# Hybrid streaming encoder on one core: where a norm's last step and statistics run, and the order of the router's products

## The chip, the cores and the metric

One core of a Trainium2 chip runs the whole program in one launch. The metric is the device time of an execution in microseconds (us). The kernel before took 1324.36 us, the median of three runs (1321.24 to 1324.84). Engines are called TensorE (PE), VectorE (DVE), ScalarE (ACT), GpSimd (POOL) and SyncE (SP), as in the profile's rows.

## The reference

One layer on 256 prompt rows and 64 sample rows of 1024 channels, all in f32. A mixing sublayer (attention and a convolution branch side by side) is followed by a layer norm, a router that chooses 4 of 32 experts for each row, the experts, and a second layer norm:

```python
x = layer_norm(DN_ALPHA * x + mix @ w_out + b_out, ln1_g, ln1_b)
logits = (x @ w_router + b_router)
top_val, top_idx = lax.top_k(logits, TOP_K)
gate = jax.nn.softmax(top_val, axis=-1)
# for each expert e and the rows xe that chose it:
gt = jnp.minimum(xe @ w_gate[e] + b_gate[e], SWIGLU_LIMIT)
up = jnp.clip(xe @ w_up[e] + b_up[e], -SWIGLU_LIMIT, SWIGLU_LIMIT)
h = gt * jax.nn.sigmoid(SWIGLU_ALPHA * gt) * (up + 1.0)
yb = h @ w_down[e] + b_down[e]
# ff: each row's four yb, weighted by gate, summed
y = layer_norm(DN_ALPHA * x + ff, ln2_g, ln2_b)

def layer_norm(x, g, b):
    mu = x.mean(-1, keepdims=True)
    var = jnp.square(x - mu).mean(-1, keepdims=True)
    return ((x - mu) * lax.rsqrt(var + LN_EPS)) * g + b
```

The weights of the 32 experts are 12.6 MB each and are read once.

## The kernel before

The rows are held in three tiles: tile 0 (prompt rows 0 to 127), tile 1 (128 to 255) and tile 2 (the 64 sample rows, laid out as two halves of 512 channels on 128 partitions). Each engine runs an instruction list of its own; named semaphores connect them, and an engine goes through its list strictly in order.

**Router.** VectorE ends the first norm of the tiles in the order 2, 0, 1 (`x1_ready`). TensorE turns each tile with transposes (`turn_x1`, L1313), ScalarE copies the turned tile (`x1T_a`), and TensorE multiplies it by the router's weights (`logits`, L1324) in the order 0, 2, 1. `keep_clock` (L1331) issues products whose result nobody reads, each with two instructions of 256 columns. VectorE's `picked` (L901 to L910) takes the four best of each row, for the tiles 0, 2, 1. Then TensorE counts the rows of each expert (L1356, L1363), VectorE makes the ranks and `at_visit` (L948), and TensorE makes three rows of the order of visits out of it (L1415 to L1419, `order_mm`). VectorE turns these into tables: `rounds_ready` (L958) is what the head of TensorE's loop reads, `tables_done` (L972) what SP, GpSimd, ScalarE and VectorE read. Between these steps TensorE gathers the rows of the first block (`gather(sel0, ...)`, L1378; tiles 0, 1 and 2 are summed in one bank), and turns the gates (L1424).

**Experts.** A visit takes one expert's weights, in 6 buffers of 4 MB (two each for gate, up and down). For each block of 32 rows TensorE runs the gate products (L1388), the up products (L1388), the gather of the next block, the down products (L1464) and the `combine` of the block before (L1405, L1407), whose result VectorE adds to `yacc` (L994, `yadd`). SP waits for `tables_done` and loads the experts half by half (`load_half`, L250) in the order of the table; a half is issued when TensorE has done with what stood in it (`gate_half`, `gate_done` and so on). Visit 0 and visit 1 are loaded before the router is done.

**Tail.** After the last block, `combine(total, tt)` for the three tiles, VectorE's sums, and the second norm. For tile 0 and tile 1 VectorE makes the statistics (`var2`, L1043 and L1045), ScalarE the root (`std2`, L689), VectorE the reciprocal (`rstd2`, L1054) and (x - mean) * g (`scaled2`, L1049). Tile 0's last step is split: ScalarE multiplies by rstd (L693, `unit2`) and GpSimd adds b (L546, `y0_ready`). Tile 1's and tile 2's last steps are VectorE's (L1074, L1080). The tile 1 sum is L1060, `yadd` count total * 3 + 5. ln2's g and b come by DMA into rows 0, 1, 5 and 6 of the weight buffer `WG[0]` (`ln2_in`). SP issues the outputs in one list:

```python
for tt in range(2):
    sp.wait_ge(sem(f"y{tt}_ready"), 1)
    sp.dma_start(y_prompt[0, P * tt:P * tt + P, :], WG[0][:, 2 + tt, :])   # L410
sp.wait_ge(sem("y2_ready"), 1)
for half in range(2):
    sp.dma_start(split(y_sample[0])[:, :, half, :], ...)                   # L413
```

Of the kernel before, what the change touches and what calls it, by code (L numbers as in the profile page):

```python
# [5 lines left out]
ALU = mybir.AluOpType  # L6
ACT = mybir.ActivationFunctionType
# [7 lines left out]
P = 128  # L15
D = 1024
# [18 lines left out]
Q = P // SLOTS  # L35
# [19 lines left out]
def encoder_step(nc, x_prompt, x_sample, cache_k, cache_v, state_conv, w_in, b_in, rel_bias, w_att_o,  # L55
# [22 lines left out]
    with ctx:  # L78
# [5 lines left out]
        PS = ctx.enter_context(nc.psum_tensor("PS", [P, 8, 512], F32))  # L84

        def view(off, *dims, rows=P):
            n = 1
            for d in dims:
                n *= d
            ap = SB[0:rows, off:off + n]  # L90
            if len(dims) == 2:
                ap = ap.rearrange("p (a b) -> p a b", a=dims[0])
            if len(dims) == 3:
                ap = ap.rearrange("p (a b c) -> p a b c", a=dims[0], b=dims[1])
            return ap
# [69 lines left out]
        M0 = S0 + 5120  # L165
        tin = view(M0, 256)
        xg = view(M0 + 256, KC, SLOTS)
        hT = view(M0 + 512, KC, SLOTS)
# [70 lines left out]
        def sem(name):  # L239
            if name not in sems:  # L240
                sems[name] = ctx.enter_context(nc.semaphore(name))
            return sems[name]
# [37 lines left out]
        def _(sp):  # L280
# [127 lines left out]
            for tt in range(2):  # L408
                sp.wait_ge(sem(f"y{tt}_ready"), 1)
                sp.dma_start(y_prompt[0, P * tt:P * tt + P, :], WG[0][:, 2 + tt, :]).then_inc(sem("y_out"), 16)  # L410
# [10 lines left out]
        def _(pool):  # L421
# [122 lines left out]
            pool.wait_ge(sem("ln2_in"), 96)  # L544
            pool.wait_ge(sem("unit2"), 1)
            pool.tensor_tensor(WG[0][:, 2, :], WG[0][:, 2, :], WG[0][:, 1, :], ALU.add).then_inc(sem("y0_ready"), 1)  # L546

        @block.scalar
        def _(act):  # L550
# [135 lines left out]

            for tt in range(3):
                act.wait_ge(sem("var2"), tt + 1)
                act.activation(rstd[:, tt:tt + 1], mv[:, tt, 1:2], ACT.Sqrt, bias=eps_c).then_inc(sem("std2"), 1)  # L689
                if tt == 0:  # L690
                    act.wait_ge(sem("scaled2"), 1)
                    act.wait_ge(sem("rstd2"), 1)
                    act.activation(WG[0][:, 2, :], WG[0][:, 2, :], ACT.Copy, scale=rstd[:, 0:1]).then_inc(sem("unit2"), 1)  # L693

        @block.vector
        def _(dve):
            n = [0]

            def link(ins):  # L700

                n[0] += 1
                ins.then_inc(sem("dve_chain"), 1)
                dve.wait_ge(sem("dve_chain"), n[0])
# [333 lines left out]

            def var2(tt):

                dve.wait_ge(sem("yadd"), total * 3 + (4 + tt))
                for s in range(2):
                    ins = dve.bn_stats(stats[:, tt, 6 * s:6 * s + 6], yacc[:, D * tt + 512 * s:D * tt + 512 * s + 512])  # L1043
                link(ins)
                dve.bn_aggr(mv[:, tt, :], stats[:, tt, :]).then_inc(sem("var2"), 1)  # L1045
                dve.wait_ge(sem("var2"), tt + 1)

            def scaled2(tt):
                dve.scalar_tensor_tensor(WG[0][:, 2 + tt, :], yacc[:, D * tt:D * tt + D], mv[:, tt, 0:1], WG[0][:, 0, :],  # L1049
                                         ALU.subtract, ALU.mult).then_inc(sem("scaled2"), 1)  # L1050

            def rstd2(tt):
                dve.wait_ge(sem("std2"), tt + 1)
                dve.reciprocal(rstd[:, tt:tt + 1], rstd[:, tt:tt + 1]).then_inc(sem("rstd2"), 1)  # L1054

            add_tile(total, 0)
            var2(0)
            dve.wait_ge(sem("comb_mm"), total * 3 + 2)
            y1 = yacc[:, D:2 * D].rearrange("p (q n) -> p q n", q=Q)
            dve.scalar_tensor_tensor(y1, PS[:, 0:4, 0:256], gcol[:, 1:2], y1, ALU.mult, ALU.add).then_inc(sem("yadd"), 1)  # L1060
            dve.wait_ge(sem("ln2_in"), 96)
            scaled2(0)
            rstd2(0)
            var2(1)
            add_tile(total, 2)
            y2 = yacc[:, 2 * D:2 * D + 512]
            dve.wait_ge(sem("yadd"), total * 3 + 6)
            link(dve.bn_stats(stats[:, 2, 0:6], y2))
            halves_aggregated("var2", 3)
            scaled2(1)  # L1070
            rstd2(1)
            dve.wait_ge(sem("scaled2"), 2)
            dve.wait_ge(sem("rstd2"), 2)
            dve.scalar_tensor_tensor(WG[0][:, 3, :], WG[0][:, 3, :], rstd[:, 1:2], WG[0][:, 1, :], ALU.mult, ALU.add).then_inc(sem("y1_ready"), 1)  # L1074

            v = WG[0][:, 4, 0:512]
            link(dve.scalar_tensor_tensor(v, y2, mv[:, 2, 0:1], WG[0][:, 5, 0:512], ALU.subtract, ALU.mult))
            rstd2(2)
# [5 lines left out]
        def _(pe):  # L1084
# [253 lines left out]
            logits(0).then_inc(sem("logit_mm"), 1)  # L1338
            keep_clock(2)
            pe.wait_ge(sem("x1T_a"), TURN_PLACE[2])  # L1340
# [71 lines left out]
            pe.wait_ge(sem("sel0_ready"), 1)  # L1412
            gather(sel0, range(2))
            pe.wait_ge(sem("at_visit_ready"), 1)
# [4 lines left out]
            pe.matmul(PS[0:1, 6, 128:128 + NV], ident[0:1, 0:1], later, start=False, stop=True).then_inc(sem("order_mm"), 1)  # L1419
            gather(sel0, range(2, 3)).then_inc(sem("gath_mm"), 1)  # L1420
            pe.wait_ge(sem("gates_ready"), 1)
# [58 lines left out]
            combine(total, 2)  # L1480

# [25 lines left out]
```

## Time and profile before

| | |
|---|---|
| median of 3 runs | 1324.36 us (1321.24 to 1324.84) |
| profiled execution, its own time | 1322.88 us |
| its span (first to last instruction) | 1321.2 us |
| TensorE busy, share of the span | 1250.5 us, 95% |
| VectorE busy | 617.6 us, 47% |
| ScalarE busy | 202.3 us, 15% |
| GpSimd busy | 140.6 us, 11% |
| read from HBM | 455.14 MB |
| granted TensorE clock, mean | 0.987 |

The spans and all times of rows are those of the profiled execution. A matmul of f32 stands as two instructions in the profile, and as many weight loads. The page cuts the span into 40 equal slices of 33 us; its lines of digits give the busy share in tenths, and one gives GB/s. "PEclk" is the granted clock of TensorE, 1.00 for 2.4 GHz and 0.50 for 1.2 GHz.

### The profile page before, as it was taken

How to read it: one execution, taken by the hardware profiler on the slowest of the kernel's cores; microseconds unless marked ns; L12 is line 12 of the kernel's file. 1: busy time of each engine (PE TensorE's matmuls, PEld its weight loads, DVE VectorE, ACT ScalarE, POOL GpSimd, SP SyncE). 2: the span in 40 equal slices, each digit the busy share in tenths (PEclk: the TensorE clock that was granted, in tenths of full speed). 3: DMA queues.
4: the chain of work that ended last, by engine and by line, in shares of the span. 5: the costliest groups of instructions: out<-in, count | busy, mean ns of one | idle time of the engine just before them, and what ended most of it. 6: DMA issues, size and time to landing. Idle time of an engine off the chain costs nothing.

```text
span 1321.2 us, 41429 instructions
## 1 busy us (share of the span) xinstructions
PE 1250.5 (95%) x16750; PEld 721.7 (55%) x16751; DVE 617.6 (47%) x1156; ACT 202.3 (15%) x380; POOL 140.6 (11%) x466
## 2 busy tenths in 40 slices
PE   8999999999999989799999999999999799999994
PEld 6777676476645545345555555555555345555552
DVE  0369995473236433344344334443444234434445
ACT  1111112343002101011111111111111111111111
POOL 1930000000001000011001100110001001100110
PEclk9999999999999999899999999999999999999997
DMA  9333334652898999999999999999999999999995
GB/s 312 105 111 123 127 127 149 164 173 83 324 416 355 428 428 428 428 428 429 429 429 429 429 429 428 429 429 429 429 429 429 429 429 429 429 429 428 429 428 209
DMA packets 69652, 459.72 MB, mean 348 GB/s; under 512 B 18284, under 2 KB 22108, under 8 KB 45017
## 3 DMA queue, kind: packets, MB, share of 16 engines
q1 hardware_dynamic: 69336, 459.03, 84.8%
q10 hardware_dynamic: 289, 0.33, 0.1%
q8 instruction: 16, 0.26, 0.1%
q14 instruction: 11, 0.09, 0.0%
HBM read 455.14 MB, written 4.73 MB: 348 GB/s over the span
## 4 chain that ended last, share of the span: by engine, by line
PE 87%; DMA 9%; DVE 2%; issue 1%; ACT 1%; POOL 0%; POOLq 0%; SPq 0%; ACTq 0%; DVEq 0%
PE PS L1388 28%; PE PS L1464 15%; PE PS L1105 13%; DMA SB<-in_w_down_dram 9%; PE PS L1378 6%; PE PS L1405 5%; PE PS L1280 3%; PE PS L1213 3%; PE PS L1168 2%; PE PS L1290 2%; PE PS L1407 2%; PE PS L1124 1%; PE PS L1134 1%; PE PS L1455 1%; PE PS L1395 1%
## 5 line engine op out<-in xcount | busy, mean ns | idle before, releaser
L1388 PE MATMUL PS<-SB 128*32 128x256 f32 x7424 | 429.1, 383 | 36.3 <-issue 15.5
L1388 PEld LDWEIGHTS PS<-SB 128*32 128x32 f32 x7424 | 236.1, 110 | 214.1 <-issue 52.6
L1464 PE MATMUL PS<-SB 128*32 128x256 f32 x3712 | 215.8, 384 | 7.4 <-DMA SB<-in_w_down_dram 7.2
L994 DVE SCALAR_TENSOR_TENSOR SB<-PS,SB 128x1024 f32<-128x1024 f32 x176 | 193.6, 1100 | 7.2 <-PE PS L1405 2.9
L1006 DVE TENSOR_SCALAR PS<-PS 128x256 f32<-128x256 f32 x58 | 25.1, 433 | 337.2 <-PE PS L1395 337.2
L1105 PE MATMUL PS<-SB 128*128 128x320 f32 x640 | 172.8, 433 | 1.3 <-ACT SB L586 1.3
L1464 PEld LDWEIGHTS PS<-SB 128*32 128x32 f32 x3712 | 115.4, 111 | 89.8 <-DVE SB L1021 10.2
L1105 PEld LDWEIGHTS PS<-SB 128*128 128x128 f32 x640 | 121.4, 190 | 51.9 <-issue 1.5
L745 DVE SCALAR_TENSOR_TENSOR SB<-SB 128x350 f32<-128x350 f32 x240 | 118.6, 573 | 0.0
L684 ACT COPY SB<-PS 128x256 f32<-128x256 f32 x58 | 21.6, 372 | 603.6 <-PE PS L1464 603.6
L1378 PE MATMUL PS<-SB 128*32 128x256 f32 (+1 forms) x1416 | 96.6, 386 | 0.0
L1405 PE MATMUL PS<-SB 32*128 32x256 f32 x944 | 84.0, 426 | 0.6 <-ACT SB L684 0.6
L1013 DVE TENSOR_SCALAR PS<-PS 128x256 f32<-128x256 f32 x58 | 25.1, 433 | 121.9 <-PE PS L1395 121.9
L535 POOL CAST SB<-SB 96x1 bf16 x58 | 10.7, 184 | 664.2 <-PE PS L1455 664.0
L682 ACT ACT_TABLE_LOAD x58 | 74.4, 1283 | 6.6 <-DVE SB L972 5.5
L1378 PEld LDWEIGHTS PS<-SB 128*32 128x32 f32 (+1 forms) x1416 | 33.7, 107 | 53.7 <-issue 43.1
L1405 PEld LDWEIGHTS PS<-SB 32*128 32x128 f32 x944 | 37.0, 183 | 38.0 <-issue 37.9
L682 ACT ACTIVATE SB<-PS 128x256 f32<-128x256 f32 x58 | 22.3, 385 | 165.9 <-DVE PS L1006 165.9
L568 ACT ACTIVATE SB<-PS,SB 128x320 f32 x40 | 21.1, 528 | 142.5 <-PE PS L1105 142.5
L1213 PE MATMUL PS<-SB 128*128 128x320 f32 x128 | 38.0, 442 | 0.0
L1034 DVE TENSOR_SCALAR SB<-PS,SB 128x320 f32<-128x320 f32 x58 | 32.0, 551 | 12.8 <-issue 12.8
L1008 DVE TENSOR_TENSOR SB<-SB,PS 128x256 f32<-128x256 f32 x58 | 24.4, 421 | 26.2 <-ACT SB L682 26.2
(245 smaller groups left out, 894.8 us busy)
## 6 DMA issues: line engine op xcount, KB each, us to landing
SB<-in_w_gate_dram SPq DMA_DIRECT2D x64, 2048.0 KB, 18.4
SB<-in_w_up_dram SPq DMA_DIRECT2D x64, 2048.0 KB, 24.0
SB<-in_w_down_dram SPq DMA_DIRECT2D x64, 2048.0 KB, 27.1
SB<-in_w_in_dram SPq DMA_DIRECT2D x13, 2048.0 KB, 7.9
SB<-in_w_pw_dram SPq DMA_DIRECT2D x2, 2048.0 KB, 8.6
SB<-in_w_att_o_dram SPq DMA_DIRECT2D x2, 2048.0 KB, 7.7
SB<-in_w_out_dram SPq DMA_DIRECT2D x2, 2048.0 KB, 9.9
SB<-in_w_in_dram SPq DMA_DIRECT2D x4, 512.0 KB, 7.6
```

Of the source, the lines that this page charges most:

```text
L682: act.activation(tin, PS[:, 0, 0:256], ACT.Sigmoid, scale=SW_ALPHA).then_inc(sem("sig"), 1)
L745: dve.scalar_tensor_tensor(yc[:, c, :], uext[:, c, bass.ds(k, CONVN)], dwT[:, c, bass.ds(k, 1)], yc[:, c, :], ALU.mult, ALU.add).then_inc( ...
L994: dve.scalar_tensor_tensor(y, ps, gcol[:, tt:tt + 1], y, ALU.mult, ALU.add).then_inc(sem("yadd"), 1)
L1034: dve.tensor_scalar(scat, PS[:, 0, 0:T], slotcol[:, bass.ds(done + b, 1)], None, ALU.is_equal).then_inc(sem("scat_ready"), 1)
L1105: ins = pe.matmul(PS[:, t, 0:T], ring[s][:, c, P * t:P * t + P], xT[:, c, :], start=(c == 0), stop=(c == KC - 1))
L1168: ins = pe.matmul(PS[:, 2 * s + tt, :], xT[:, c, t0:t0 + r], ring[s][:, c, :], start=(c == 0), stop=(c == KC - 1))
L1213: ins = pe.matmul(PS[:, 6 + j % 2, 0:T], ring[s][:, c, P * t:P * t + P], zc[:, c, :], start=(c == 0), stop=(c == KC - 1))
L1280: ins = pe.matmul(PS[:, t % 4, 0:T], ring[s][:, c, P * (t % 4):P * (t % 4) + P], oT[:, c, :], start=(c == 0), stop=(c == KC - 1))
L1378: ins = pe.matmul(PS[32 * q:32 * q + 32, 3, 0:256], sel[r, tt, :], x_part(tt, q // 2)[:, k], start=(tt == 0), stop=(tt == 2))
L1388: ins = pe.matmul(PS[32 * q:32 * q + 32, bank, 0:256], xg[:, c, :], buf[:, c, 256 * q:256 * q + 256], start=(c == 0), stop=False)
L1405: ins = pe.matmul(PS[:, bank + q, 0:256], scat[r, P * tt:P * tt + P], ysb[r, :], start=True, stop=True)
L1464: ins = pe.matmul(PS[32 * n:32 * n + 32, 2, 256:512], hT[:, ck, :], WD[par][:, ck, 256 * n:256 * n + 256], start=(ck == 0), stop=(ck == KC ...
```

## The change

In the tail, tile 0's last step goes to TensorE: ScalarE makes `unit_diag`, the identity scaled by tile 0's rstd, and TensorE computes, for each half of 512 channels, a ones row times b plus `unit_diag` times the scaled tile 0, into banks 0 and 1. ScalarE copies both halves to the output rows, and `y0_ready` now counts two. GpSimd only sets the ones row. Tile 1's mean and variance go from VectorE to ScalarE: a copy scaled by -1/D with an accumulator, a square about that mean with an accumulator, and the root. VectorE's remaining steps are done in another order: tile 2's (x - mean) * g before tile 1's.

In the router, `keep_clock(2)` between the logits of tile 0 and of tile 2 is left out, and the order products stand behind the gather of tile 0 alone; the gather of tile 1 goes behind them, beside that of tile 2.

```diff
+        unit_diag = view(M0, P)
+        ones_row = WG[0][0:1, 5, 512:512 + P]
...
             for tt in range(2):
-                sp.wait_ge(sem(f"y{tt}_ready"), 1)
+                sp.wait_ge(sem(f"y{tt}_ready"), 2 - tt)
...
             pool.wait_ge(sem("ln2_in"), 96)
-            pool.wait_ge(sem("unit2"), 1)
-            pool.tensor_tensor(WG[0][:, 2, :], WG[0][:, 2, :], WG[0][:, 1, :], ALU.add).then_inc(sem("y0_ready"), 1)
+            pool.memset(ones_row, 1.0).then_inc(sem("ones_set"), 1)
...
-            for tt in range(3):
-                act.wait_ge(sem("var2"), tt + 1)
+            def std2(tt, count):
+                act.wait_ge(sem("var2"), count)
                 act.activation(rstd[:, tt:tt + 1], mv[:, tt, 1:2], ACT.Sqrt, bias=eps_c).then_inc(sem("std2"), 1)
-                if tt == 0:
-                    act.wait_ge(sem("scaled2"), 1)
-                    act.wait_ge(sem("rstd2"), 1)
-                    act.activation(WG[0][:, 2, :], WG[0][:, 2, :], ACT.Copy, scale=rstd[:, 0:1]).then_inc(sem("unit2"), 1)
+            std2(0, 1)
+            y1, spare = yacc[:, D:2 * D], WG[0][:, 7, :]
+            act.wait_ge(sem("yadd"), total * 3 + 5)
+            act.activation(spare, y1, ACT.Copy, scale=-1.0 / D, accum_out=mv[:, 1, 0:1]).then_inc(sem("mean1"), 1)
+            act.wait_ge(sem("mean1"), 1)
+            act.activation(spare, y1, ACT.Square, bias=mv[:, 1, 0:1], accum_out=mv[:, 1, 1:2]).then_inc(sem("square1"), 1)
+            act.wait_ge(sem("square1"), 1)
+            act.activation(rstd[:, 1:2], mv[:, 1, 1:2], ACT.Sqrt, bias=eps_c, scale=1.0 / D).then_inc(sem("std2"), 1)
+            act.wait_ge(sem("rstd2"), 1)
+            act.activation(unit_diag, ident, ACT.Copy, scale=rstd[:, 0:1]).then_inc(sem("diag_ready"), 1)
+            std2(2, 2)
+            for h in range(2):
+                act.wait_ge(sem("unit_mm"), h + 1)
+                act.copy(WG[0][:, 2, 512 * h:512 * h + 512], PS[:, h, :]).then_inc(sem("y0_ready"), 1)
...
             rstd2(0)
-            var2(1)
             add_tile(total, 2)
...
-            halves_aggregated("var2", 3)
-            scaled2(1)
+            halves_aggregated("var2", 2)
+            v = WG[0][:, 4, 0:512]
+            dve.scalar_tensor_tensor(v, y2, mv[:, 2, 0:1], WG[0][:, 5, 0:512], ALU.subtract, ALU.mult).then_inc(sem("scaled2"), 1)
+            dve.wait_ge(sem("mean1"), 1)
+            dve.scalar_tensor_tensor(WG[0][:, 3, :], y1, mv[:, 1, 0:1], WG[0][:, 0, :], ALU.add, ALU.mult).then_inc(sem("scaled2"), 1)
             rstd2(1)
...
-            v = WG[0][:, 4, 0:512]
-            link(dve.scalar_tensor_tensor(v, y2, mv[:, 2, 0:1], WG[0][:, 5, 0:512], ALU.subtract, ALU.mult))
             rstd2(2)
...
             logits(0).then_inc(sem("logit_mm"), 1)
-            keep_clock(2)
             pe.wait_ge(sem("x1T_a"), TURN_PLACE[2])
...
             pe.wait_ge(sem("sel0_ready"), 1)
-            gather(sel0, range(2))
+            gather(sel0, range(1))
             pe.wait_ge(sem("at_visit_ready"), 1)
...
-            gather(sel0, range(2, 3)).then_inc(sem("gath_mm"), 1)
+            gather(sel0, range(1, 3)).then_inc(sem("gath_mm"), 1)
...
             combine(total, 2)
 
+            pe.wait_ge(sem("ones_set"), 1)
+            pe.wait_ge(sem("yadd"), total * 3 + 5)
+            pe.wait_ge(sem("scaled2"), 1)
+            pe.wait_ge(sem("diag_ready"), 1)
+            for h in range(2):
+                k = slice(512 * h, 512 * h + 512)
+                pe.matmul(PS[:, h, :], ones_row, WG[0][0:1, 1, k], start=True, stop=False)
+                pe.matmul(PS[:, h, :], unit_diag, WG[0][:, 2, k], start=False, stop=True).then_inc(sem("unit_mm"), 1)
```

## Rows read from the trace of the kernel before

**Rows 1.** The page, its slices: GB/s moved in each of 40.

```profile
GB/s 312 105 111 123 127 127 149 164 173 83 324 416 355 428 428 428 428 428 429 429 429 429 429 429 428 429 429 429 429 429 429 429 429 429 429 429 428 429 428 209
```

**Rows 2.** The chain of waits, 380 to 440: start us, us, what.

```profile
398.47 0.94 PE PS L1331 x4
399.42 1.05 PE PS L1324 x32
...
403.81 0.20 DVE SB L901
...
408.39 1.00 PE PS L1378 x16
```

**Rows 3.** The timeline, 388 to 424: start, us, engine, line, operation, count [idle before].

```profile
397.65 1.29 DVE L875 SCALAR_TENSOR_TENSOR SB<-SB 128x1024 f32<-128x1024 f32 x1
...
402.39 0.19 DVE L910 TENSOR_TENSOR SB<-SB 128x32 bf16<-128x32 f32 x1
...
408.73 0.24 DVE L948 TENSOR_SCALAR SB<-SB 32x46 f32<-32x46 f32 x1
...
412.56 3.66 PE L1388 MATMUL PS<-SB 128*32 128x256 f32 x64 [1.28 <-issue]
...
414.71 2.91 SPq L250 DMA_DIRECT2D SB<-in_w_gate_dram  x2
```

**Rows 4.** Single lines, TensorE's queue: last wait before the loop, its first instruction.

```profile
L1429 PEldq EVENT_SEMAPHORE  x1: 51/51/51, 410.6 to 410.6; - x1
...
L1430 PEldq MOVE  x1: 29/29/29, 410.9 to 410.9; - x1
```

**Rows 5.** Windows: us, busy of PE, PEld, DVE, ACT, POOL, clock, DMA share, GB/s.

```profile
413.50:414.00 0.50, 0.50 (x16) 0.34 (x12) 0.50 (x1) 0.24 (x1) 0.00 (x0) 1.00 0.00 0
```

**Rows 6.** The timeline of the tail, 1302 to 1322.

```profile
1304.88 0.48 PE L1407 MATMUL PS<-SB 32*64 32x128 f32 x16 [0.97 <-DVE SB L994]
...
1306.52 1.28 DVE L1060 SCALAR_TENSOR_TENSOR SB<-PS,SB 128x1024 f32<-128x1024 f32 x1
...
1308.98 1.27 DVE L1043 BATCH_NORM_STATS2 SB<-SB 128x6 f32<-128x512 f32 x2
1309.16 1.15 ACT L693 ACTIVATE SB<-SB 128x1024 f32<-128x1024 f32 x1 [2.44 <-DVE SB L1054]
1310.28 0.21 DVE L1045 BATCH_NORM_AGGREGATE SB<-SB 128x2 f32<-128x12 f32 x1
...
1312.83 3.58 SPq L410 DMA_DIRECT2D out_dram<-SB  x2
...
1316.93 0.75 DVE L1080 SCALAR_TENSOR_TENSOR SB<-SB 128x512 f32<-128x512 f32 x1
1317.71 1.26 SPq L413 DMA_DIRECT2D out_dram<-SB  x2
```

**Rows 7.** Timelines of other stretches, for the duration of one kind of instruction.

```profile
225.80 1.28 ACT L600 ACT_TABLE_LOAD   x1
...
289.40 0.19 ACT L612 ACTIVATION_READ_ACCUMULATOR SB<-SB 128x1 f32 x1
...
291.19 0.56 ACT L622 COPY SB<-PS 128x512 f32<-128x512 f32 x1
...
387.49 7.03 PE L1290 MATMUL PS<-SB 128*128 128x512 f32 x16
```

**Rows 8.** Windows where the granted clock changes; columns as in rows 5.

```profile
548.40:548.80 0.40, 0.40 (x8) 0.20 (x4) 0.00 (x0) 0.00 (x0) 0.00 (x0) 0.64 1.07 451
...
1306.40:1306.60 0.20, 0.00 (x0) 0.00 (x0) 0.09 (x1) 0.17 (x1) 0.00 (x0) 0.61 0.00 0
```

**Rows 9.** The timeline of TensorE, 538 to 570.

```profile
545.93 3.26 PE L1388 MATMUL PS<-SB 128*32 128x256 f32 x32 [2.96 <-DMA SB<-in_w_gate_dram]
```

**Rows 10.** Windows near the end, while only tile 2's output is under way.

```profile
1319.00:1319.50 0.50, 0.00 (x0) 0.00 (x0) 0.00 (x0) 0.00 (x0) 0.00 (x0) 0.50 0.88 200
```

**Rows 11.** DMA issues, 1260 to 1322: KB each, median us from issue to landing.

```profile
out_dram<-SB SPq DMA_DIRECT2D x2, 512.0 KB, 2.6
```

More of the change, by code:

```diff
@@ L1037, in _ @@
             total = dve.value_load(tbl[0:1, NV:NV + 1], min_val=1, max_val=200)
[L1039 to L1050, printed above, removed]
             def rstd2(tt):
@@ L1056, in _ @@
             add_tile(total, 0)
-            var2(0)
+            dve.wait_ge(sem("yadd"), total * 3 + 4)
+            for s in range(2):
+                ins = dve.bn_stats(stats[:, 0, 6 * s:6 * s + 6], yacc[:, 512 * s:512 * s + 512])
+            link(ins)
+            dve.bn_aggr(mv[:, 0, :], stats[:, 0, :]).then_inc(sem("var2"), 1)
+            dve.wait_ge(sem("var2"), 1)
             dve.wait_ge(sem("comb_mm"), total * 3 + 2)
-            y1 = yacc[:, D:2 * D].rearrange("p (q n) -> p q n", q=Q)
-            dve.scalar_tensor_tensor(y1, PS[:, 0:4, 0:256], gcol[:, 1:2], y1, ALU.mult, ALU.add).then_inc(sem("yadd"), 1)
+            y1 = yacc[:, D:2 * D]
+            dve.scalar_tensor_tensor(y1.rearrange("p (q n) -> p q n", q=Q), PS[:, 0:4, 0:256], gcol[:, 1:2],
+                                     y1.rearrange("p (q n) -> p q n", q=Q), ALU.mult, ALU.add).then_inc(sem("yadd"), 1)
             dve.wait_ge(sem("ln2_in"), 96)
-            scaled2(0)
+            dve.scalar_tensor_tensor(WG[0][:, 2, :], yacc[:, 0:D], mv[:, 0, 0:1], WG[0][:, 0, :],
+                                     ALU.subtract, ALU.mult).then_inc(sem("scaled2"), 1)
             rstd2(0)
-            var2(1)
             add_tile(total, 2)
@@ L1068, in _ @@
             link(dve.bn_stats(stats[:, 2, 0:6], y2))
-            halves_aggregated("var2", 3)
-            scaled2(1)
+            halves_aggregated("var2", 2)
[3 more added lines that the diff above has]
+            dve.scalar_tensor_tensor(WG[0][:, 3, :], y1, mv[:, 1, 0:1], WG[0][:, 0, :], ALU.add, ALU.mult).then_inc(sem("scaled2"), 1)
             rstd2(1)
-            dve.wait_ge(sem("scaled2"), 2)
+            dve.wait_ge(sem("scaled2"), 3)
             dve.wait_ge(sem("rstd2"), 2)
             dve.scalar_tensor_tensor(WG[0][:, 3, :], WG[0][:, 3, :], rstd[:, 1:2], WG[0][:, 1, :], ALU.mult, ALU.add).then_inc(sem("y1_ready"), 1)
-            v = WG[0][:, 4, 0:512]
-            link(dve.scalar_tensor_tensor(v, y2, mv[:, 2, 0:1], WG[0][:, 5, 0:512], ALU.subtract, ALU.mult))
             rstd2(2)
```

## The prediction

> **What bounds the kernel.** I read the 40 slices of the page first. The reader is to see the GB/s line [rows 1]: from the fourteenth slice to the last but one it stands at 428 or 429. The weights of the experts are streamed without a pause for some 890 us, and whatever TensorE does in those microseconds, the stream ends so long after it began. So a microsecond is won in three places: before the stream begins, in the stream's bytes (unchanged), and in the tail behind it. The change touches the first and the third. I then read the chain of waits around the router [rows 2], the timeline there [rows 3] for who is free when, TensorE's queue at the loop's head [rows 4], and one window of DMA [rows 5].
>
> The stream begins at 414.71, when SP issues a half of the gate weights into the buffer that visit 0 reads. It waits for half of visit 0's gate products, which start at 412.56 [rows 3]. The DMA engines moved nothing from 413.5 to 414.0 [rows 5]: what had been loaded ahead had landed. So the hole closes by as much as visit 0 starts earlier, and everything behind moves with it, rigidly. This holds while the gain is under the roughly 2 us for which the queue is empty.
>
> **Router, the idle products.** Two products are removed between the logits of tile 0 and of tile 2: 0.94 us on TensorE [rows 2]. Is this time on the path? Logits of tile 2 would run from 398.47 to 399.5 instead of from 399.42 to 400.5 [rows 2]. The turn of tile 1 needs its norm, done at 397.65 + 1.29 = 398.94 [rows 3]: earlier than 399.5, no new wait. The logits of tile 1 then end 0.94 earlier. VectorE takes them at 403.81 [rows 2], and it has been done with tile 2 since 402.39 + 0.19 = 402.58 [rows 3]: 1.23 us of slack, more than 0.94. All of the 0.94 passes, and I know of no row that excludes some 0.1 of loss at a hand-over: 0.8 to 0.94.
>
> **Router, order products sooner.** Before, 16 instructions of the gather (tiles 0 and 1) took 1.00 us from 408.39 and the order products started right behind, at 409.39 [rows 2]. Their input is there at 408.73 + 0.24 = 408.97 [rows 3]. With eight instructions ahead, TensorE is free at 408.9, waits 0.1, and starts them at 409.03: 0.36 us sooner, and VectorE's table chain behind them by as much. TensorE's own work before the loop grows by the 0.14 that it waits. Visit 0 starts when the loop's head has read the table: its first instruction ran at 410.9, but the queue had already passed the wait ahead of it at 410.6 [rows 4], so only 0.3 lay between table and queue, and eight more products and their weight loads now stand in the queue behind the order products. Visit 0 gains between 0 and 0.36; I take 0.15, since the queue's own arrival (0.3 sooner at most, less the 0.14) is the nearer limit. Router together: -0.94 - 0.15 = **-1.1 us**, bounds -0.8 and -1.3.
>
> **Tail, VectorE.** Off VectorE go tile 1's two statistics and their aggregation, from 1308.98 to 1310.53, about 1.5 us [rows 6]. The rest keeps its form and changes order. Its last operation starts at 1316.93 today and would start near 1315.4; y2 is ready near 1316.1 and y1 near 1315.2. If nothing else were in the way the tail would end 1.5 us sooner. The output copies hang on one SP queue in the order y0, y1, y2, and the question is y0.
>
> **Tail, y0.** Today: ScalarE scales tile 0 (1.15 us, from 1309.16), GpSimd adds the bias, and SP issues y0 at 1312.83 [rows 6]. After: ScalarE first does tile 1. Its sum is written at 1306.52 + 1.28 = 1307.80. Copy and square over 1024 elements, each 1.15 like the scaling [rows 6] and 0.19 to read the accumulator [rows 7], make 2.7; the root of one column and the scaled identity of 128 have no row of their own shape here; together they lie between nothing and two 512-column copies at 0.56 [rows 7], I take 0.7. That gives 1311.2 for diag_ready (1310.5 to 1311.6, no matter beside what follows). All four products wait for it, also the two with the ones row, which don't need it, because they stand in the queue behind that wait.
>
> The price of the products: four of 512 columns in f32 are eight instructions. 16 such instructions took 7.03 us [rows 7], so eight cost 3.5 us at the full clock. But the granted clock in the tail is not full. TensorE's last product today ends at 1304.88 + 0.48 = 1305.4 [rows 6], and the clock falls between 1306.4 and 1306.6 (mean 0.61, then 0.50) [rows 8]. So the products start at the lower level, 1.2 GHz, where eight cost 7.0: 32 instructions of L1388 took 3.26 us after a pause of 2.96 us [rows 9] where 64 took 3.66 in the loop [rows 3]. In that case the clock came back inside 548.4 to 548.8 (mean 0.64) [rows 8], 2.8 us after the restart at 545.93. If it comes back likewise, 2.8 us of the 7.0 are done slowly and the rest takes 2.1: 4.9. It may come later, or not within 7.0 us. I take 5.3; bounds 3.5 (full clock throughout, which the rows speak against) and 7.0.
>
> The Trainium skill ("TensorE: Matmul & The Clock Gate", Part 1: The HAM clock gate) says that the throttled state is the default and that activity releases it, so that work put on an idle TensorE is dear at first. The trace agrees in the restart at 545.93. By its rule alone the products cost more than 3.5 and the tail cannot win its 1.5; the sum above goes by the rows.
>
> So the products end at 1311.2 + 5.3 = 1316.5, the last copy of 512 columns at 1317.1, and y0 is issued there, 4.3 us later than today. y1 (ready 1315.2) and y2 (1316.1) are queued behind it on SP. The three now run one after another: 512 KB take 1.2 us each at the 428 GB/s [rows 1], y2's 256 KB take 1.3 at the 200 GB/s seen when it alone was under way [rows 10], together 3.7; one 512 KB output took 2.6 from issue to landing [rows 11], of which 1.4 is not data; and 0.4 stood behind the last landing (second half of y2 issued near 1318.4, landed 2.4 later, span 1321.2 [rows 6]). The end is 1317.1 + 3.7 + 1.4 + 0.4 = 1322.6 against 1321.2: **+1.4 us**. With 3.5 for the products it is 1320.8 (-0.4), with 7.0 it is 1324.3 (+3.1). GpSimd's ones row needs only the bias rows, and its wait on tile 0 is gone: no cost. On the queue of ScalarE the root of tile 2 stands behind tile 1's pass; it is needed when VectorE has finished y1, some 3 us later: no cost.
>
> **Sum.** -1.1 + 1.4 = +0.3 us: the two parts cancel. The profiled execution took 1322.88 for a span of 1321.2 (1.7 around it), so it would take 1323.2. The median of the runs lies 1.5 above that execution, so the forecast of a median is 1324.36 + 0.3, about **1324.6 us**. A measurement of this kernel can tell about 0.3% from no change, which is 4.0 us here.
>
> **Rivals.**
> (a) *The clock stays low for all eight instructions*: tail +3.1, sum +2.0, 1326.4 us. For it: the products come after 5.8 us of idleness against 2.96 in the row [rows 9]. Against: there it came back in 2.8. 0.17.
> (b) *TensorE is at its full clock*: tail -0.4, sum -1.5, 1322.9 us. Against it the fall at 1306.4 to 1306.6 [rows 8]; it would take an activity that the tail doesn't have. 0.04.
> (c) *The router's gain doesn't arrive* because a stall of the stream absorbs it, or SP isn't ready for its first load: sum +1.4, 1325.8 us. Against it the empty window [rows 5] and the flat GB/s line [rows 1]. 0.10.
> (e) *Faster by over 0.3%*: it needs 4 us and both parts together can give only 1.3 + 1.5 = 2.8, even with y0 free. Only the scatter of the runs (1321.24 to 1324.84) could show it. 0.04.
>
> **How the numbers follow.** Forecast 0.61, (a) 0.17, (b) 0.04, (c) 0.10, (d) 0.04, (e) 0.04. The forecast and (a) to (c) lie within 0.3%. Faster is (e) and a 0.01 of (b), 0.05; slower is (d), 0.04; the rest, 0.91, is within 0.3%. The range: from the lowest sum (-1.7) to that of (a) with the smaller router gain (+2.3), that is 1322.7 to 1326.7 about the median, and the runs of one kernel differ by up to 3.6 us, a median by less; I add 1.5 and 1 to it: 1321.0 to 1327.7.
>
> **What would show it.** In the profile after: logits of tile 1 end 0.9 sooner; VectorE's table chain 1.2 to 1.3 sooner; SP's first expert load near 413.6; the line of GB/s as flat as before. In the tail: no table load between ScalarE's root and Square; the four products start with diag_ready near 1310.1 (1311.2 less the router's 1.1), with a granted clock of 0.5 and a rise inside them; y0 issued behind y1_ready, three outputs back to back at the end. The prediction is wrong if the first load isn't sooner, if the products take 3.5 us, or if y1's output leaves before VectorE's last operation ends.

## The result, and the profile after

The changed kernel took 1327.28 us, the median of 14 runs (1324.35 to 1329.39), beside 1322.98 us for the kernel before in as many (1320.97 to 1325.46). The ratio is 1.0027, 95% interval 1.0018 to 1.0036: about 3.6 us slower, clear of noise. That is near the 0.3% that I had called no difference, and the interval reaches past it; the two medians alone are 4.3 us apart. The forecast of 1324.6 lies 2.7 us under the median, which is inside the range of 1321.0 to 1327.7, 0.4 us from its upper end. In the profiles both halves went worse than forecast: the router gave +0.6 where I had -1.1, the tail +4.1 where I had +1.4.

The runs of the changed kernel lie in two groups, six from 1324.4 to 1325.9 and eight from 1327.1 to 1329.4. The profiled execution (span 1326.3, its own time 1328.05) is one of the upper group.

I read the router in the timeline first. All starts are 0.37 later here before anything of the change has run (the turn of tile 0 starts at 394.73 instead of 394.36), so I count from that turn, called T. Before, it was this row:

```profile
394.36 1.44 PE L1313 MATMUL PS<-SB 128*128 128x128 f32 x16
```

And in the changed kernel:

```profile
394.73 1.44 PE L1318 MATMUL PS<-SB 128*128 128x128 f32 x16
...
396.87 3.30 PE L1329 MATMUL PS<-SB 128*128 128x32 f32 x48
...
400.09 1.97 PE L1318 MATMUL PS<-SB 128*128 128x128 f32 x8
...
404.76 0.19 DVE L913 TENSOR_TENSOR SB<-PS,SB 128x32 f32<-128x32 f32 x1 [1.81 <-PE PS L1329]
...
409.67 0.23 DVE L960 TENSOR_SCALAR SB<-SB 32x46 f32<-32x46 f32 x1
...
409.96 0.24 PE L1419 MATMUL PS<-SB 32*1 32x46 f32 x2
...
411.73 0.45 DVE L974 STREAM_TRANSPOSE SB<-PS 128x256 f32<-128x256 f32 x1 [0.19 <-PE PS L1382]
...
413.38 0.18 DVE L984 CAST SB<-SB 1x46 int32<-1x46 f32 x1
...
413.52 3.66 PE L1392 MATMUL PS<-SB 128*32 128x256 f32 x64 [1.04 <-issue]
...
415.68 2.72 SPq L252 DMA_DIRECT2D SB<-in_w_gate_dram  x2
```

The same stretch in windows, the granted clock third from the end:

```profile
398.50:399.00 0.50, 0.50 (x12) 0.46 (x13) 0.50 (x1) 0.00 (x0) 0.00 (x0) 1.00 1.07 459
399.00:399.50 0.50, 0.50 (x24) 0.50 (x22) 0.47 (x2) 0.00 (x0) 0.14 (x1) 0.95 1.15 492
399.50:400.00 0.50, 0.50 (x14) 0.50 (x10) 0.43 (x5) 0.00 (x0) 0.33 (x4) 0.50 1.07 459
...
402.00:403.00 1.00, 1.00 (x6) 0.82 (x4) 0.85 (x4) 0.89 (x2) 0.00 (x0) 0.57 0.89 377
```

The reader is to see the 48 logit instructions without the idle products between them, and then the clock at 0.50 from 399.5 to 402.5, although TensorE was busy in every one of these windows. The turn of tile 1 takes 1.97 us. VectorE gets the logits of tile 1 at T + 10.03, against 403.81 - 394.36 = T + 9.45 before [rows 2]: 0.58 later instead of 0.94 sooner. The first expert load is issued at T + 20.95 instead of 414.71 - 394.36 = T + 20.35 [rows 3].

The tail, in the timeline. I count from the start of tile 0's last combine, called C; it is 1302.77 before and 1303.82 here. Two rows of before are needed beside it:

```profile
1302.77 1.15 PE L1405 MATMUL PS<-SB 32*128 32x256 f32 x16 [0.57 <-ACT SB L684]
...
1312.13 0.70 DVE L880 COPY SB<-SB 64x6 f32<-64x6 f32 x1
```

And the changed kernel:

```profile
1303.82 1.15 PE L1409 MATMUL PS<-SB 32*128 32x256 f32 x16 [0.57 <-ACT SB L685]
...
1308.89 1.06 ACT L695 ACTIVATE SB<-SB 128x1024 f32<-128x1024 f32 x1 [1.11 <-DVE SB L1064]
...
1310.07 1.15 ACT L697 ACTIVATE SB<-SB 128x1024 f32<-128x1024 f32 x1
...
1311.53 0.17 DVE L892 COPY SB<-SB 64x6 f32<-64x6 f32 x1
1311.54 0.39 ACT L701 ACTIVATE SB<-SB 128x128 f32<-128x128 f32 x1
...
1312.07 2.04 PE L1492 MATMUL PS<-SB 1*128 1x512 f32 x2 [5.66 <-ACT SB L701]
...
1312.83 1.28 DVE L1078 SCALAR_TENSOR_TENSOR SB<-SB 128x1024 f32<-128x1024 f32 x1
...
1314.04 2.08 PE L1493 MATMUL PS<-SB 128*128 128x512 f32 x2
...
1314.29 1.28 DVE L1082 SCALAR_TENSOR_TENSOR SB<-SB 128x1024 f32<-128x1024 f32 x1
...
1315.68 0.75 DVE L1085 SCALAR_TENSOR_TENSOR SB<-SB 128x512 f32<-128x512 f32 x1
...
1318.05 2.08 PE L1493 MATMUL PS<-SB 128*128 128x512 f32 x2
...
1320.16 0.58 ACT L705 COPY SB<-PS 128x512 f32<-128x512 f32 x1 [3.42 <-PE PS L1493]
1320.77 0.83 SPq L412 DMA_DIRECT2D out_dram<-SB  x2
1321.65 2.09 SPq L415 DMA_DIRECT2D out_dram<-SB  x2
```

And the clock there, in windows:

```profile
1312.00:1313.00 1.00, 0.93 (x1) 0.49 (x2) 0.96 (x3) 0.29 (x1) 0.00 (x0) 0.50 0.00 0
...
1319.00:1320.00 1.00, 1.00 (x2) 0.00 (x0) 0.00 (x0) 0.00 (x0) 0.00 (x0) 0.50 0.00 0
```

The four products run from 1312.07 to 1320.13, 8.06 us, all of it at 0.50. VectorE is done at 1316.43 and y1 is ready at 1315.57, but y0 is issued only at 1320.77 = C + 16.95 (before C + 10.06 [rows 6]), and y1 and y2 behind it. The span ends at C + 22.48 against C + 18.43.

The 5.1 us between the two spans are so accounted for: 0.37 ahead of the router, 0.60 in it, 0.08 between the first load and C, 4.05 in the tail. From first load to C it was 888.06 us before (1302.77 - 414.71) and 888.14 after.

### The profile page after: what moved, and what is told of

It is laid out like the page before. It is cut to its first block, busy times and chain, and to the rows that moved or that the text cites. A ratio compares the mean times of both kernels' runs of the same rounds, so it can differ in the third digit from the quotient of the medians.

```text
span 1326.3 us, 41439 instructions
## 1 busy us (share of the span) xinstructions
PE 1261.0 (95%) x16754; PEld 725.3 (55%) x16755; DVE 615.3 (46%) x1153; ACT 204.9 (15%) x386; POOL 138.1 (10%) x466
## 4 chain that ended last, share of the span: by engine, by line
PE 87%; DMA 9%; issue 1%; DVE 1%; ACT 1%; POOL 0%; POOLq 0%; SPq 0%; ACTq 0%; DVEq 0%
PE PS L1392 28%; PE PS L1468 15%; PE PS L1110 13%; DMA SB<-in_w_down_dram 9%; PE PS L1382 6%; PE PS L1409 5%; PE PS L1285 3%; PE PS L1218 3%; PE PS L1173 2%; PE PS L1295 2%; PE PS L1411 2%; PE PS L1129 1%; PE PS L1139 1%; PE PS L1459 1%; PE PS L1399 1%
```

## The experiments

T and C are as above. A router is read by the issue of the first expert load, a tail by its end, both from the profile, because the runs of one kernel differ by more than the sizes in question.

**1. The two idle products back** (`r_keep`).

```diff
             logits(0).then_inc(sem("logit_mm"), 1)
+            keep_clock(2)
             pe.wait_ge(sem("x1T_a"), TURN_PLACE[2])
```

> The changed kernel with the two idle products put back between the logits of tile 0 and tile 2; everything else as changed. Theory C (clock): the changed kernel lost its router gain because TensorE fell to 0.50 from 399.4 to 402.6, while it turned tile 1 (1.97 us for eight transposes instead of 1.09) and multiplied. With the products back the clock stays at 1.00, the head of tile 1's take-over by VectorE stands 0.6 us earlier after the first turn than in the changed kernel (from the turn of tile 0 at 394.36 to VectorE's tile 1 step at 403.81 it was 9.45 before, and 10.03 after), so about 9.45 here. Rival (phase): the clock falls here too, and the stretch is 10.4 or more. The whole kernel: 0.5 to 1 us under the changed one, about 3 us over the kernel before, since the tail is as changed.

Measured: the clock stayed at 1.00 through the router, with VectorE's step at T + 9.45 and the first load at T + 20.39. The ratio to before was 1.0026 (1.0017 to 1.0035), as the changed kernel's: timing can't see the router. The tail was the changed one, 22.5 us with the products 8.05. Of the router's change the order of the products is what is left here: 0.04 us, in the wrong direction.

**2. Only the idle products left out of the kernel before** (`r_idle_only`).

```diff
             logits(0).then_inc(sem("logit_mm"), 1)
-            keep_clock(2)
             pe.wait_ge(sem("x1T_a"), TURN_PLACE[2])
```

> The kernel before with only the two idle products left out. Theory C: the clock falls during tile 1's turn in some or all executions; where it falls, VectorE's tile 1 step comes 0.5 to 0.6 us later than in the kernel before (stretch from the first turn 10.0), where it doesn't, 0.9 earlier (8.5). Prediction's theory: always 8.5, and the whole kernel 0.9 us faster. The whole kernel lies within 1 us of the kernel before either way, which timing alone can't tell; the profile decides.

Measured: ratio 1.0003 (0.9994 to 1.0012). The profile holds both theories in one execution. These are rows of its timeline, then two of its windows.

```profile
399.52 1.09 PE L1313 MATMUL PS<-SB 128*128 128x128 f32 x8
...
411.77 5.35 PE L1387 MATMUL PS<-SB 128*32 128x256 f32 x64 [1.37 <-issue]
...
415.58 0.35 SPq L250 DMA_DIRECT2D SB<-in_w_gate_dram  x1
```

```profile
412.00:412.50 0.50, 0.50 (x8) 0.23 (x4) 0.50 (x2) 0.00 (x0) 0.00 (x0) 0.50 0.08 33
...
415.00:415.50 0.50, 0.50 (x12) 0.30 (x8) 0.00 (x0) 0.00 (x0) 0.32 (x2) 0.72 0.00 0
```

The turn of tile 1 ran at full speed and the logits came at T + 8.51: the 0.94 of my sum, whole. But then the clock fell at visit 0. Its windows from 411.5 to 415.5 read 0.87, 0.50 (six times) and 0.72, the first 64 gate instructions took 5.35 us instead of 3.66 [rows 3], and since half of them release the first load, that was issued at T + 21.16, 0.8 later than before. So my expectation was half right: the clock can fall in two places.

The other kernels' profiles bear on the same question. Without the idle products it fell around the turn of tile 1 in five (the changed kernel and experiments 3, 7, 8 and 11; first load at T + 20.89 to T + 20.98), at visit 0 in one (this one), and not at all in one (experiment 4: first load at T + 19.50). With them it never fell, in six profiles (before, experiments 1, 5, 6, 9 and 10; T + 20.35 to T + 20.39).

**3. TensorE kept at work in the tail** (`t_warm`). The results of the added products are not used.

```diff
+            for _ in range(6):
+                pe.matmul(PS[:, 4, 0:256], ident, WU[0][:, 0, 0:256], start=True, stop=True)
             combine(total, 2)
...
             pe.wait_ge(sem("scaled2"), 1)
+            for _ in range(6):
+                pe.matmul(PS[:, 2, 0:256], ident, WU[0][:, 0, 0:256], start=True, stop=True)
             pe.wait_ge(sem("diag_ready"), 1)
```

> The changed kernel with idle products of 256 columns on TensorE in the tail: six before the last combine, six after it, into banks that nobody reads then. Their results are not used. Theory C: TensorE never pauses, the clock stays at 1.00 and the four products take 3.5 us instead of 8.06, so y0 is issued 4.5 us sooner and the kernel is about 4 us faster than the changed one, within 0.5 us of the kernel before or under it. Rival (the price is the instruction's own: a one-row or a diagonal operand costs 1.0 us an instruction at any clock): 8 us again, no gain.

Measured: ratio 1.0006 (0.9997 to 1.0015). Its timeline, with the second six of the added products first:

```profile
1309.46 2.83 PE L1492 MATMUL PS<-SB 128*128 128x256 f32 x12 [0.99 <-DVE SB L1067]
...
1312.22 1.12 PE L1496 MATMUL PS<-SB 1*128 1x512 f32 x2
...
1313.27 1.12 PE L1497 MATMUL PS<-SB 128*128 128x512 f32 x2
...
1315.38 1.13 PE L1497 MATMUL PS<-SB 128*128 128x512 f32 x2
...
1317.15 0.83 SPq L412 DMA_DIRECT2D out_dram<-SB  x2
```

The clock was 1.00 and the four took 1312.22 to 1316.51, 4.3 us. So the clock is what the 8.06 are made of, and the instruction's own price at full clock is 1.05 us a product here, not the 0.88 that I took from rows 7. y0 went out at C + 14.06, 2.9 us sooner than in the changed kernel where I expected 4.5, and the end was C + 19.5, 1.1 us later than before. Most of that 1.1 is the experiment's own: the added products ended only at 1312.29, so the four started at C + 9.13 instead of C + 8.25. Without these 0.9 us the end would be near C + 18.6, an estimate from the two starts: 0.2 later than before. So the prediction's rival (b), which gave the tail -0.4 at full clock, was too kind to the change by some 0.6.

**4. The bias over 128 rows instead of one** (`t_full_rows`).

```diff
-                pe.matmul(PS[:, h, :], ones_row, WG[0][0:1, 1, k], start=True, stop=False)
+                pe.matmul(PS[:, h, :], ident, WG[0][:, 1, k], start=True, stop=False)
```

> The changed kernel, but the bias comes through the identity times 128 rows of b (the bias rows are the same on all partitions) instead of a ones row times one row of b: same number of products and columns. Theory C1 (TensorE's activity during the four products is too thin because two of them use one row of the array): the clock comes back 3 to 4 us after the start and the four take 5.5 to 6 us, the kernel 2 to 2.5 us faster than changed. Rival C2 (rows don't matter; after such a long pause it comes back late or by chance): 8.06 us again, no change, or a mixture from run to run as in the changed kernel, whose runs lie in two groups around 1325 and 1327.6.

Measured: ratio 1.0009 (1.0000 to 1.0019). Its timeline and its windows:

```profile
1308.67 2.05 PE L1492 MATMUL PS<-SB 128*128 128x512 f32 x2 [5.66 <-ACT SB L701]
...
1312.21 1.21 PE L1492 MATMUL PS<-SB 128*128 128x512 f32 x2
...
1313.26 1.02 PE L1493 MATMUL PS<-SB 128*128 128x512 f32 x2
```

```profile
1312.00:1312.50 0.50, 0.50 (x2) 0.29 (x1) 0.46 (x3) 0.04 (x1) 0.00 (x0) 0.50 0.00 0
1312.50:1313.00 0.50, 0.50 (x2) 0.22 (x2) 0.50 (x1) 0.50 (x1) 0.00 (x0) 0.91 0.00 0
```

After the same pause of 5.66 us the clock came back at about 1312.5, 3.9 us after the start, and the four products ended at 1314.28: 5.6 us, the end at C + 20.0. With the same columns and all rows of the array in use in all four products, the clock came back, where it did not with two one-row products among the four, in the profiles of the changed kernel and of experiments 1 and 8. That is one profile of this kernel, which can't exclude chance by itself. Its ten runs (1321.68 to 1325.75) agree with it: eight of them lie below the fastest of experiment 1, which was measured with it and has the changed tail, and these eight show a mean granted clock of 0.987 to 0.991, against 0.984 to 0.986 in all of experiment 1. In the other two it was 0.984, so the clock seems not to come back in every execution.

**5. Tile 1's statistics on ScalarE alone** (`t_stats_only`). The router and tile 0's last step are those of before.

```diff
+            act.wait_ge(sem("scaled2"), 1)
             act.wait_ge(sem("rstd2"), 1)
-            act.activation(unit_diag, ident, ACT.Copy, scale=rstd[:, 0:1]).then_inc(sem("diag_ready"), 1)
+            act.activation(WG[0][:, 2, :], WG[0][:, 2, :], ACT.Copy, scale=rstd[:, 0:1]).then_inc(sem("unit2"), 1)
...
+            pool.wait_ge(sem("unit2"), 1)
+            pool.tensor_tensor(WG[0][:, 2, :], WG[0][:, 2, :], WG[0][:, 1, :], ALU.add).then_inc(sem("y0_ready"), 1)
```

> The kernel before with one part of the tail's change alone: tile 1's mean and variance on ScalarE and VectorE's new order. Tile 0's last step stays with ScalarE's scaling and GpSimd's addition, now behind tile 1's statistics on ScalarE; the router is that of before. Theory: the statistics are the half that pays and the products the half that costs. Counted from the start of tile 0's last combine (C): y0 issued at C + 11.3 instead of C + 10.1, y1 at C + 11.8 instead of C + 13.3, y2 ready at C + 12.6, three outputs nearly back to back, end at C + 16.8 instead of C + 18.4. The kernel is 1.6 us faster than before, 1320.8 where that is 1322.4, and over 5 us faster than the changed one. Rival (outputs back to back on SP are the cost, whoever makes y0): end at C + 18 or later.

Measured: ratio 0.9996 (0.9987 to 1.0005), end at C + 18.2 instead of the C + 16.8 expected. y0 came as expected (C + 11.4), y1 did not (C + 13.9). The number is that of the rival (C + 18 or later), but not by its reason: SP issued y0 at 1313.64 and then waited some 2.5 us for y1, so the outputs weren't back to back. The timeline shows why y1 was late:

```profile
1311.27 2.34 POOL L548 TENSOR_TENSOR SB<-SB 128x1024 f32<-128x1024 f32 x1 [25.75 <-ACT SB L703]
1311.29 3.41 DVE L1077 SCALAR_TENSOR_TENSOR SB<-SB 128x1024 f32<-128x1024 f32 x1
...
1314.87 1.28 DVE L1081 SCALAR_TENSOR_TENSOR SB<-SB 128x1024 f32<-128x1024 f32 x1
```

VectorE's step over two SBUF inputs started 0.02 behind GpSimd's addition and took 3.41 us; its twin at 1314.87 took 1.28. It seems to have stood for GpSimd's 2.3 us and then to have run; experiment 10 tests that.

**6. The repaired tail** (`t_warm_first`), with the router's idle products back as in experiment 1.

```diff
+            for _ in range(6):
+                pe.matmul(PS[:, 4, 0:256], ident, WU[0][:, 0, 0:256], start=True, stop=True)
             combine(total, 2)
...
             pe.wait_ge(sem("scaled2"), 1)
+            for h in range(2):
+                pe.matmul(PS[:, h, :], ones_row, WG[0][0:1, 1, 512 * h:512 * h + 512], start=True, stop=False)
             pe.wait_ge(sem("diag_ready"), 1)
             for h in range(2):
                 k = slice(512 * h, 512 * h + 512)
-                pe.matmul(PS[:, h, :], ones_row, WG[0][0:1, 1, k], start=True, stop=False)
                 pe.matmul(PS[:, h, :], unit_diag, WG[0][:, 2, k], start=False, stop=True).then_inc(sem("unit_mm"), 1)
```

> The changed kernel with three repairs: the router's two idle products back, six idle products of 256 columns ahead of the last combine, and both ones-row products ahead of the wait for the scaled identity. Theory: the clock is 1.00, the ones rows run while ScalarE makes the statistics, and only two products of 1.05 us stand behind diag_ready: y0 issued at C + 11.0, end at C + 16.6 (before C + 18.4, changed C + 22.5). About 1.8 us faster than before. Rival: the pause between combine and products lets the clock fall again, end at C + 18.6 or more, no gain over before.

Measured: ratio 0.9988 (0.9979 to 0.9996), median 1320.40 beside 1322.70. Its timeline:

```profile
1301.68 1.15 PE L1410 MATMUL PS<-SB 32*128 32x256 f32 x16 [0.57 <-ACT SB L685]
...
1308.05 1.95 PE L1493 MATMUL PS<-SB 1*128 1x512 f32 x4 [1.00 <-DVE SB L1067]
...
1309.93 1.98 PE L1497 MATMUL PS<-SB 128*128 128x512 f32 x4
...
1312.56 1.24 SPq L412 DMA_DIRECT2D out_dram<-SB  x2
...
1314.32 1.27 SPq L415 DMA_DIRECT2D out_dram<-SB  x2
```

y0 at C + 10.9, end at C + 16.3, 2.1 us sooner than before. Two products in a row with the same weights took 1.95 and 1.98 us, where an alternating pair in experiment 3 took 2.17 (1312.22 to 1314.39). This version is faster than both kernels, than the one before by 0.12% (0.04% to 0.21%).

**7. The ones rows first, nothing else** (`t_ones_first`): the second hunk of experiment 6 alone.

> The changed kernel with only the two ones-row products moved ahead of the wait for the scaled identity. The clock is expected at 0.50 all through, since the first two products use one row of the array: they take from C + 6.3 to C + 10.3, the other two end at C + 14.3 instead of C + 16.3, end of the kernel at C + 20.5, 2 us faster than changed. If rows of the array don't matter to the clock, it comes back inside and the end is C + 18.5.

Measured: ratio 1.0019 (1.0009 to 1.0029), end at C + 20.0. The products ran from 1308.28 to 1315.73, and y0 went out at C + 14.5 instead of C + 16.95. The clock was 0.50 until 1315.6, 0.1 before the last of them ended. The end lies between my two expectations, nearer to the first (C + 20.5 with the clock low all through; C + 18.5 with the clock back in time): the order is worth 2.5 us, and the clock came back too late to matter. It came back 7.3 us after the first one-row product and 3.7 us after the first with 128 rows (1311.95), which goes with experiment 4. The ten runs spread over 6.0 us (1322.14 to 1328.17), the profiled one (1323.68) among the faster, so one profile doesn't stand for all of them.

**8. The outputs in the order y1, y2, y0** (`t_y0_last`).

```diff
-            for tt in range(2):
-                sp.wait_ge(sem(f"y{tt}_ready"), 2 - tt)
...
+            prompt_out(1)
+            sp.wait_ge(sem("y2_ready"), 1)
...
+            prompt_out(0)
```

> The changed kernel with SP's outputs in the order y1, y2, y0. Theory: y1 and y2, ready at C + 11.8 and C + 12.6, no longer wait behind y0, and only its 2.6 us and 0.4 stand behind the last copy: end at C + 20.0 instead of C + 22.5 with the low clock. If SP's order is not a cost, C + 22.5 as before. Also a further look at the router without the idle products: the clock falls during tile 1's turn or just behind it in three of four so far.

Measured: ratio 1.0013 (1.0004 to 1.0022), end at C + 19.9 with the products at the low clock (8.06 us). SP's order was worth 2.5 us of the tail's 4.05.

**9. Only the order products sooner** (`r_order_only`), one execution, so without a ratio.

```diff
-            gather(sel0, range(2))
+            gather(sel0, range(1))
             pe.wait_ge(sem("at_visit_ready"), 1)
...
-            gather(sel0, range(2, 3)).then_inc(sem("gath_mm"), 1)
+            gather(sel0, range(1, 3)).then_inc(sem("gath_mm"), 1)
```

> The kernel before with only the order products ahead of the gather of tile 1. Counted from the turn of tile 0 (T): the table chain's last step began at T + 18.23 before and begins at T + 18.08 here; visit 0's products at T + 18.20 before and T + 18.24 here; the first expert load at T + 20.35 before and T + 20.39 here, because the transposition of the gathered rows now waits for the gather. So no gain where it counts. Prediction's theory: visit 0 0.15 us sooner, T + 18.05.

Measured: the tables' last step at T + 18.07, visit 0 at T + 18.21, the first load at T + 20.36. No gain.

**10. GpSimd's addition behind tile 1's last step** (`t_add_late`), experiment 5 with one wait more; again one execution.

```diff
             pool.wait_ge(sem("unit2"), 1)
+            pool.wait_ge(sem("y1_ready"), 1)
```

> The kernel with tile 1's statistics on ScalarE and tile 0's last step on ScalarE and GpSimd, with one more wait: GpSimd's addition only begins when VectorE has finished tile 1. Theory (collision): VectorE's step over two SBUF inputs of 1024 took 3.41 us instead of 1.28 because GpSimd's addition of two SBUF inputs ran beside it; without it beside, it takes 1.28 and y1 is ready at C + 11.8 instead of C + 13.9, while the 512-element last step of tile 2 (0.75), which the addition now overlaps, is stretched to 1.5 or more. Rival (the step is slow for another reason, as its new place or its wait): 3.4 us again. y0 is later here, so the whole kernel isn't faster.

Measured, in its timeline:

```profile
1311.33 1.28 DVE L1078 SCALAR_TENSOR_TENSOR SB<-SB 128x1024 f32<-128x1024 f32 x1
...
1314.18 0.75 DVE L1085 SCALAR_TENSOR_TENSOR SB<-SB 128x512 f32<-128x512 f32 x1
...
1314.25 2.88 POOL L549 TENSOR_TENSOR SB<-SB 128x1024 f32<-128x1024 f32 x1 [28.67 <-DVE SB L1082]
```

The step took 1.28 and y1 was ready at C + 11.75: the overlap with the addition is what had cost 2.1 us. The second half of what I expected was wrong in its direction. VectorE's last step began 0.07 before the addition and kept its 0.75; the addition was the one that took longer, 2.88 instead of 2.34.

The Trainium skill ("SBUF — State Buffer", SBUF: two separate sides) says that a VectorE operation with two SBUF inputs and a GpSimd operation that reads SBUF exclude each other for a whole instruction, and that whichever starts first has its way. The two traces agree in both directions and roughly in size: VectorE's step took 2.13 us longer behind an addition of 2.34, the addition 0.54 longer behind a step of 0.75.

**11. The repaired tail without the router's idle products** (`best_no_idle`).

```diff
             logits(0).then_inc(sem("logit_mm"), 1)
-            keep_clock(2)
             pe.wait_ge(sem("x1T_a"), TURN_PLACE[2])
```

> The kernel with the repaired tail (idle products ahead of the last combine, ones rows first), but without the router's two idle products: the router as in the changed kernel. Theory: the clock falls near tile 1's turn or near visit 0 in most executions and the first load comes at about T + 20.95 to 21.2 instead of T + 20.4, in the others at T + 19.5. The mean is within 0.5 us of the kernel with the idle products, 1320.2 to 1321.2 where that stood at 1320.4, with a wider spread. Prediction's theory: 0.9 us faster in every run.

Measured: ratio 0.9984 (0.9975 to 0.9993), which experiment 6's overlaps. The clock fell at the turn of tile 1, and the first load stood at T + 20.94. Timing doesn't tell the two apart; the prediction's theory, 0.9 us in every run, is excluded by the profile.

## Why the prediction held, and where its steps failed

- **The number held in part by luck.** I added my +0.3 to 1324.36, the median of three runs of the kernel before; its median over 14 runs is 1322.98, 1.4 us lower. From there the forecast would be 1323.3 and the same range 1319.6 to 1326.3, with the measured 1327.28 outside. In the profiles both halves lie beyond the bounds that I had given them: the router at +0.6 (bounds -1.3 and -0.8) and the tail at +4.05 (highest +3.1). What held was the direction and the 0.3%, and that only just. The range has a slip besides: 1322.7 less 1.5 is 1321.2, not 1321.0. And I counted the whole of rival (d) as slower by over 0.3%, though by my own words it is that only together with the low clock.
- **The stream moves rigidly with its first load: right.** From first load to C, twelve of the thirteen traces give 887.7 to 888.4 us, and that of experiment 9 gives 889.7, so the stream itself can differ by 1.6 us from one execution to another. What the router gives or loses arrives whole. Rival (c) is out.
- **The idle products, -0.94: wrong.** The failed step is "All of the 0.94 passes". The critical path was as I had it, and where the clock held, the gain was there to the hundredth (T + 8.51, experiment 2). What I left out is what the products are for. I had named the clock as the price of the tail's products and had not asked the same of the router, whose windows all read 1.00 before. Without them the clock fell somewhere ahead of the first load in six of seven profiles, with them in none of six, which leaves little to chance. The balance is +0.5 to +0.8 us in the six and -0.85 in the seventh.
- **The order products, -0.15: mis-sized, 0 measured** (experiments 1 and 9: +0.04 and +0.01). They did start sooner: the timeline has them 0.29 behind the start of their input's step, where before it was 0.59 (408.73 [rows 3] to 409.32). The tables ended 0.15 sooner, less than the 0.36 that I gave VectorE: the transposition of the gathered rows, which before followed VectorE's own work without a wait, now waits 0.19 for the gather (row of 411.73 above). Visit 0 gained nothing of it. My lower bound, 0, is what came.
- **VectorE's 1.5 us: right, and more.** y1 was ready at C + 11.75 (13.27 before), y2 at C + 12.6 (14.9 before), where I had 12.4 and 13.3. Another 0.5 came from the copy of 64 x 6 elements (L892), 0.17 where the same one took 0.70 beside GpSimd's addition, which is gone: it took 0.69 to 0.70 in the three profiles in which the addition ran beside it (before, experiments 2 and 9) and 0.17 in the other ten. I had counted GpSimd's part as free.
- **diag_ready: right** (1311.54 + 0.39 = 1311.93, C + 8.1; forecast C + 8.4). No table load stood before Square, and rival (d) is out.
- **The products, 5.3 us: mis-sized, 8.06 measured**, above my upper bound of 7.0. Two errors add up. I took the return of the clock from rows 8 and 9, where other products had gone ahead of it (128 rows, 256 columns, one after another), and in this kernel it did not come back at all (rival (a)); and I took the price of a product from 16 in one accumulation, 0.88 at full clock, where a product here costs 1.05 (experiment 3) and 2.0 at the lower clock.
- **Behind y0's issue, 5.5 us: right** (1326.3 - 1320.77 = 5.5). That a late y0 holds up y1 and y2 on SP was the right mechanism, and experiment 8 confirms it.
- **The sum.** Forecast +0.3 us, the ratio says +3.6 (2.4 to 4.8). The tail's half of the error is the clock and the price of the products; the router's is the clock again.

**What stays open.** What of TensorE's work holds the clock or brings it back isn't shown beyond what the profiles have: in the router the fall went with four instructions of 128 x 256 more or less, and in the tail the return went with one-row or full products, in one profile each of experiments 4 and 7. Why a product of the tail costs 1.05 where one of rows 7 costs 0.88 isn't shown; that the same weights in a row cost less (experiment 6) is a part of it at most. The two groups of the changed kernel's runs are 2.8 us apart by their medians. Their mean granted clocks differ too, 0.984 to 0.987 in the faster group and 0.981 to 0.984 in the slower. A router whose clock holds would explain 1.45 us of it (T + 19.50 against T + 20.95); where the rest comes from isn't shown.

## What to carry to other kernels

Before taking out idle work on TensorE, ask what clock the next few microseconds get, and profile several executions, since the fall can come in another place or not at all. Before giving an idle engine the last step of something, price it at the lower clock, put ahead of its wait all that doesn't need the wait, and look at what is queued behind its result. An addition on GpSimd isn't free for VectorE: here a step over two SBUF operands (1.28 to 3.41) and a copy of 64 x 6 elements (0.17 to 0.70) took longer beside it. And before adding a small difference to a base, measure the base often enough: three runs put it 1.4 us too high here.

## What the runs showed of the hardware that I had not expected

- The granted clock fell while TensorE was busy all the time: 0.50 from 399.5 to 402.5 in the changed kernel, during 48 logit instructions of 32 columns and the eight transposes behind them.
- Four products of 512 columns, two of them with one row, ran for 8.05 to 8.06 us at 0.50 in three profiles; with 128 rows in all four the clock came back after 3.9 us in one.
- A VectorE step of 1.28 us took 3.41 beside a GpSimd addition that had started 0.02 earlier, and a GpSimd addition of 2.34 took 2.88 beside a VectorE step that had started 0.07 earlier.
